# Stick-breaking attention with both heads in one step, half blocks of projections between the steps, and gate projections between the banded units

## The chip, the cores and the metric

The kernel runs on one core of one Trainium2 chip. The metric is the device time of one execution in microseconds (us), taken as the median over runs. A core has five engines that run their own instruction queues in order and wait for one another through semaphores: TensorE (PE, matmuls; its weight loads are shown as PEld), VectorE (DVE), ScalarE (ACT), GpSimd (POOL) and SyncE (SP, which here issues the DMAs). PE writes to PSUM, eight banks of 128 x 512 float32 values.

## The reference

Two transformer blocks follow each other on 1024 positions of width 1024. The first has two layers (banded attention, a gated linear recurrence, memory attention, an MLP each). The change touches only the second block, whose one layer mixes two kinds of attention:

```python
proj = h @ w_in[l]
sb_q, sb_k, sb_v, sb_g, sw_q, sw_k, sw_v, sw_g = jnp.split(proj, offsets, axis=-1)
y_sb = stick_breaking_attention(sb_q, sb_k, sb_v) * jax.nn.silu(sb_g)      # 8 heads of 64
y_sw = sliding_window_sink_attention(sw_q, sw_k, sw_v, sinks) * jax.nn.silu(sw_g)
y = jnp.concatenate([y_sb, y_sw], axis=-1) @ w_out[l]
...
# stick-breaking, s < t only
log_beta = jax.nn.log_sigmoid(z)
log_1mb = jnp.where(causal, jax.nn.log_sigmoid(-z), 0.0)
later = lax.cumsum(log_1mb, axis=3, reverse=True) - log_1mb
w = jnp.where(causal, jnp.exp(log_beta + later), 0.0)
```

## The kernel before

Every tensor that feeds a projection is kept in two float32r parts (high and low), so a projection block (128 output features, all of K = 1024) is 8 x 3 matmuls for each 512 positions: 48 for both halves, 24 for a half block. Weights come in blocks of 512 KB: a DMA into `raw` (`NR` slots), then `split` makes the two parts with an ACT copy and a DVE subtraction into `wsp` (`NS` = 3 slots), two blocks ahead of use (`LA` = 2, called from `piece`). The list `order` gives the order of all blocks.

Nothing reorders the work: `Queues.add` appends each operation to its engine's queue in the order in which the program is written, and each engine executes its queue strictly in that order. An operation's `*after` arguments are the operations that it waits for. So a wait holds whatever is written behind it on the same engine.

Around the change the program of before runs, one stage after the other: projections of the stick-breaking queries (`SQ`), keys (`SK`, 4 blocks), values (`SV`) and gates (`SG`, 4 blocks; the gate is silu through Tanh, line 138 is the ACT helper `A`); a barrier; the stick-breaking steps; a barrier; the projections of the banded queries (`WQ`, 4 blocks), keys (`WK`), values (`WV`) and gates (`WG`, 4 blocks); a barrier; 16 banded units (`attention_units` on `window_units`); and the output projection.

A stick-breaking step of before is one head, one block of 128 keys and up to 512 queries (128, 256 or 384 on the diagonal). There are 96. Its stages, each several steps behind the one before, are: scores z on PE (float32, 64 rows of the array); `min` on DVE; Exp and Ln on ACT; a maximum on DVE, which gives softplus(z); its high part on POOL and low part on DVE; two triangular matmuls that add the sum within the block onto z; two matmuls with a constant matrix (`onesN`) into a carry bank of the head; a copy and an addition, Exp on ACT, and the values matmul (64 columns of the array).

`attention_units` issues for unit u: the scores of u, their maximum on DVE, the Exps; then the normalisation of u-1 (DVE reciprocal, two multiplications on DVE and two on POOL); the values of u-2; the transposes of u-1 and their copies; and last, where `fills[u]` is above 0, a half block from `fill`.

`ln_exp()` loads the ACT table set that holds both Exp and Ln; where a function that the current set lacks comes up, the compiler puts an `ACT_TABLE_LOAD` in front of it.

Of the kernel before, what the change touches and what calls it, by code (L numbers as in the profile page):

```python
# [13 lines left out]
KB = 1024  # L14
# [99 lines left out]
def program(nc, D, out, stop=None, dbg=None):  # L114
    ctx = ExitStack()
    with ctx:
# [34 lines left out]
        NR, NS, LA = 4, 3, 2  # L151
# [58 lines left out]
        blocks("in2", range(26))  # L210
# [135 lines left out]

        def half_chunks(name, bank, rhs, evac):

            def chunk(n, hf):
                b = at[0]  # L350
                assert at[1] == 0
                piece(name)
                cs = slice(512 * hf, 512 * hf + 512)
                ps = PS[:, bank, :]
                for k in range(8):
                    w = wsp[:, b % NS, :, k * 128:k * 128 + 128]
                    rh, rl, ops = rhs(k)
                    for i, (wi, r) in enumerate(((0, rh), (0, rl), (1, rh))):
                        op = mm(ps, w[:, wi, :], r[:, cs], k == 0 and i == 0, k == 7 and i == 2, splits[b], ops,
                                free[bank] if k == 0 and i == 0 else None)  # L360
                if hf == 1:
                    uses[b] = [op]
                    at[0] = b + 1
                free[bank] = [evac(n, cs, ps, op)]

            return [lambda n=n, hf=hf: chunk(n, hf) for n in range(8) for hf in range(2)]
# [348 lines left out]
        def window_units(Qt, Kt, Vt, pairs, tiles, nbs, outf, bias, sinkv):  # L715
            units = []
            for n in range(8):
                for kp in range(pairs):
                    kbs = [n + d for d in nbs if 0 <= n + d < 8]
                    for half in range(2):  # L720

                        def s(j, ps, fr, n=n, kp=kp, kbs=kbs, half=half):
                            m = ps.shape[1] // 2
                            heads = [(par, m * j + t, par * m + t) for t in range(m) for par in range(2)]
                            for par, t, i in heads:
                                rows = slice(64 * par, 64 * par + 64)
                                mm(ps[:, i, :], Qt[rows, kp * tiles + 2 * half + t, n * 128:(n + 1) * 128],
                                   Kt[rows, kp, kbs[0] * 128:(kbs[-1] + 1) * 128], t == m * j, False, fr,
                                   skip_group_check=True)
# [4 lines left out]
                        def pv(pts, ob, fr, n=n, kp=kp, kbs=kbs, half=half):  # L734
                            for j, (pt, c) in enumerate(pts):
                                for par in range(2):
                                    st = Vt[:, kbs[j], kp, 64 * par:64 * par + 64]
                                    o = mm(ob[64 * par:64 * par + 64, 256 * half:256 * half + 256], st,
                                           pt[:, 256 * par:256 * par + 256], j == 0, j == len(pts) - 1, c,
# [499 lines left out]
        SK = place(48 * KB, [128, 4, 1024])  # L1239
        SV = place(64 * KB, [128, 8, 4, 128])  # L1240
        SG = place(0, [128, 4, 1024])
        gt = place(88 * KB, [128, 2, 1024])
        sv_free = [o, *r12[0], *r12[1], *tused]

        project("in2", 4, 8, Hk, copy_to(SK, up1))
        Q.add("act", None, *sv_free)
        project_rows("in2", 4, 8, Hk, rows_to(SV, False, *sv_free))
        for e_ in ("act", "dve"):
            Q.add(e_, None, *sp2)
        gfree = [None, None]  # L1250

        def gate_to(T):
            def ev(n, p, ps, op):
                t = gt[:, n % 2, :]
                a = A(t, ps, ACT.Tanh, op, gfree[n % 2], scale=0.5)
                o = STT(T[:, n, :], t, 1.0, ps, ALU.add, ALU.mult, a)
                gfree[n % 2] = o
                return [o], None
            return ev

        project("in2", 4, 8, Hk, gate_to(SG))
# [3 lines left out]
        me = [place(o_ * KB, [128, 512]) for o_ in (28, 30, 94)]  # L1265
        sps = place(16 * KB, [128, 3, 2, 512], F32R)
        tw = place(88 * KB, [128, 3, 512])
        triI, onesN = triR[:, 0, :], triR[:, 1, :]
        ZB, AB, OBK = (0, 1, 2, 3), (4, 5), (6, 7)
        steps = []  # L1270
        grp = 0
        for pr in range(4):
            for hf in range(2):
                top = 4 * hf + 3
                for kb in range(top, -1, -1):
                    for par in range(2):
                        steps.append((pr, hf, kb, par, top, grp))
                grp += 1
        n_s = len(steps)
        F = [dict() for _ in range(n_s)]  # L1280
        got = lambda s, key: F[s].get(key) if s >= 0 else None

# [288 lines left out]
```

How the kernel before makes its waits and increments, by code:

```python
            def run(eng):  # L93
                seen = {}
                for o in self.q[name]:
                    for d in o.deps:
                        if seen.get(d.sem.name, 0) < d.val:
                            eng.wait_ge(d.sem, d.val)
                            seen[d.sem.name] = d.val
                    if o.fn is None:
                        continue
                    ins = o.fn(eng)
                    if o.sem is not None:
                        ins.then_inc(o.sem, 1 if o.sem is self.sems.get(name) else 16)
```

## Time and profile before

| | us |
|---|---|
| median of 3 runs | 3436.37 (3432.55 to 3443.11) |
| profiled execution, own time | 3448.24 |
| its span, first to last instruction | 3446.5 |
| mean granted TensorE clock over the span | 0.969 |
| steps of stick-breaking, 2830.45 to 3094.24 | 263.8 |
| banded units, 3216.78 to 3341.14 | 124.4 |

In a timeline a row gives the start, the length, the engine, the line, the operation with its output and inputs, and a count; in brackets stands how long the engine had been idle and what released it. Rows of the same kind that follow each other are merged. A float32 matmul appears as two records, a float32r or bfloat16 matmul as one. The granted clock is 1.0 at 2.4 GHz and 0.5 at 1.2 GHz. Line 279 is the matmul helper, 138 the ACT helper, 141, 144, 148 and 149 are DVE helpers; buffers placed by `place` are all called p in the trace.

### The profile page before, as it was taken

The numbers are of one execution on the slowest core, as the hardware profiler recorded it, in microseconds if no ns is written. First come the engines' busy times: TensorE is split into PE (matmuls) and PEld (weight loads), VectorE is DVE, ScalarE is ACT, GpSimd is POOL, SyncE is SP. The second block draws the span as 40 slices with busy tenths as digits, with TensorE's granted clock in tenths as the row PEclk, the third lists the DMA queues.
The fourth block names the chain that finished last, engine by engine and source line by source line (L and its number), as shares of the span: only waits on it lengthen the run. The fifth ranks groups of instructions, "written<-read, shape, count | busy, mean of one in ns | idle before, by whom it ended". The sixth has DMA issues, their size and how long they took to land.

```text
span 3446.5 us, 35176 instructions
## 1 busy us (share of the span) xinstructions
PE 3220.3 (93%) x14288; PEld 2446.3 (71%) x14298; DVE 1706.5 (50%) x2254; ACT 1095.1 (32%) x1853; POOL 261.4 (8%) x258
## 2 busy tenths in 40 slices
PE   4999989999999999999799999999997999999768
PEld 4777557778888888777577788888875874448546
DVE  6544864444444433699644433333345326771355
ACT  4202652311111111488423111111125226761332
POOL 0001431000000000000010000000003002220120
PEclk9999999999999999999899999999998998999799
DMA  4211010122222211211211111111111310001012
GB/s 167 98 37 31 1 56 31 37 74 74 68 73 74 71 46 55 70 46 49 98 37 43 43 49 49 45 48 49 49 50 53 112 37 1 1 19 43 13 68 92
DMA packets 52865, 186.01 MB, mean 54 GB/s; under 512 B 5856, under 2 KB 6240, under 8 KB 52576
## 3 DMA queue, kind: packets, MB, share of 16 engines
q1 hardware_dynamic: 52704, 183.76, 16.2%
q8 instruction: 113, 1.85, 0.2%
q14 instruction: 48, 0.39, 0.0%
HBM read 169.06 MB, written 13.63 MB: 53 GB/s over the span
## 4 chain that ended last, share of the span: by engine, by line
PE 79%; DVE 9%; ACT 7%; issue 2%; POOL 2%; DMA 0%; DVEq 0%; ACTq 0%; POOLq 0%; SPq 0%
PE PS L279 77%; ACT p L138 5%; DVE p L141 3%; PE PS L517 2%; DVE sm L482 1%; DVE p L144 1%; POOL p L508 1%; DVE p L1091 1%; ACT H L138 1%; DVE wsp L141 0%; ACT wsp L138 0%; DVE p L530 0%; ACT L138 0%; DVE p L398 0%; DVE sm L144 0%
## 5 line engine op out<-in xcount | busy, mean ns | idle before, releaser
L279 PE MATMUL PS<-H,wsp 128*128 128x512 f32 x6864 | 1596.5, 393 | 39.7 <-POOL H L1189 21.2
L279 PEld LDWEIGHTS PS<-H,wsp 128*128 128x128 f32 x6864 | 1292.7, 189 | 328.2 <-ACT p L138 25.3
L279 PE MATMUL PS<-p,wsp 128*128 128x512 f32 (+1 forms) x3840 | 896.6, 394 | 42.1 <-DVE p L141 21.6
L279 PEld LDWEIGHTS PS<-p,wsp 128*128 128x128 f32 x3840 | 714.7, 191 | 219.9 <-ACT wsp L138 37.8
L138 ACT ACTIVATE p<-p 128x512 f32<-128x512 f32 (+5 forms) x522 | 355.1, 690 | 860.3 <-DVE p L144 677.3
L138 ACT ACTIVATE wsp<-raw 128x1024 fp32r<-128x1024 f32 (+1 forms) x262 | 271.3, 1039 | 778.0 <-PE PS L279 637.5
L141 DVE TENSOR_TENSOR p<-p,PS 128x1024 f32<-128x1024 f32 (+4 forms) x280 | 251.5, 898 | 505.8 <-PE PS L279 500.0
L141 DVE TENSOR_TENSOR wsp<-raw,wsp 128x1024 fp32r<-128x1024 f32 (+1 forms) x262 | 317.7, 1215 | 200.7 <-ACT wsp L138 200.7
L279 PE MATMUL PS<-p 128*64 128x256 f32 (+9 forms) x1432 | 385.1, 486 | 18.7 <-DVE p L144 5.2
L141 DVE TENSOR_TENSOR p<-PS,p 128x1024 f32<-128x1024 f32 (+1 forms) x124 | 143.0, 1154 | 442.7 <-PE PS L279 417.4
L508 POOL TENSOR_SCALAR p<-p,sm 128x256 f32<-128x256 f32 (+2 forms) x128 | 150.6, 1181 | 1912.1 <-DVE sm L501 1912.1
L141 DVE TENSOR_TENSOR p<-p 128x1024 f32<-128x1024 f32 (+8 forms) x283 | 239.2, 847 | 108.5 <-ACT p L138 106.8
L279 PEld LDWEIGHTS PS<-p 128*64 128x64 f32 (+2 forms) x1432 | 154.5, 177 | 143.4 <-ACT p L138 62.1
L138 ACT ACTIVATE p<-PS 128x512 f32<-128x512 f32 (+4 forms) x245 | 135.6, 573 | 342.1 <-PE PS L279 315.8
L138 ACT ACTIVATE p<-PS,sm 128x256 f32<-128x256 f32 (+2 forms) x256 | 127.9, 508 | 266.9 <-DVE sm L148 137.4
L517 PE MATMUL PS<-cf,p 128*128 128x128 f32 x600 | 97.0, 300 | 77.9 <-POOL p L508 66.0
L144 DVE SCALAR_TENSOR_TENSOR p<-p 128x1024 f32<-128x1024 f32 (+1 forms) x119 | 143.3, 1215 | 20.3 <-ACT p L138 17.8
L517 PEld LDWEIGHTS PS<-cf,p 128*128 128x128 f32 x600 | 72.0, 152 | 114.0 <-issue 63.4
L482 DVE TENSOR_REDUCE sm<-PS 128x2 f32<-128x768 f32 (+3 forms) x96 | 94.9, 989 | 64.8 <-PE PS L279 64.3
L149 DVE TENSOR_SCALAR p<-PS 128x512 f32<-128x512 f32 (+4 forms) x105 | 61.6, 587 | 93.7 <-PE PS L279 93.6
L1341 POOL CAST p<-p 128x512 fp32r<-128x512 f32 (+3 forms) x96 | 69.7, 726 | 344.3 <-ACT p L138 159.6
L279 PE MATMUL PS<-p,triR 128*128 128x512 f32 (+3 forms) x352 | 94.6, 385 | 0.3
(69 smaller groups left out, 1313.7 us busy)
## 6 DMA issues: line engine op xcount, KB each, us to landing
raw<-in_dn_dram SPq DMA_DIRECT2D x68, 512.0 KB, 3.5
raw<-in_in_dram SPq DMA_DIRECT2D x66, 512.0 KB, 3.6
raw<-in_up_dram SPq DMA_DIRECT2D x64, 512.0 KB, 3.6
raw<-in_out_dram SPq DMA_DIRECT2D x40, 512.0 KB, 3.5
p<-in_ada_dram SPq DMA_DIRECT2D x24, 512.0 KB, 4.5
raw<-in_kv_dram SPq DMA_DIRECT2D x16, 512.0 KB, 3.9
p<-in_x_dram SPq DMA_DIRECT2D x16, 512.0 KB, 9.0
spill_dram<-p SPq DMA_DIRECT2D x16, 512.0 KB, 2.9
```

What stands on the lines that cost most here:

```text
L138: return act(lambda e: e.activation(o, i, f, **kw), *a)
L141: return dve(lambda e: e.tensor_tensor(o, x, y, op), *a)
L144: return dve(lambda e: e.scalar_tensor_tensor(out=o, in0=x, scalar=s, in1=y, op0=op0, op1=op1), *a)
L149: return dve(lambda e: e.tensor_scalar(o, x, s1, s2, op0, op1), *a)
L279: return pe(lambda e: e.matmul(o, l, r, start=start, stop=stop, **kw), *a)
L482: o = dve(lambda e: e.tensor_reduce(mx, S, AX.X, ALU.max), op, prev)
L508: last[1] = pool(lambda e, P_=P_, r=r: e.tensor_scalar(P_, P_, r, None, ALU.mult), o)
L517: o = pe(lambda e, t_out=t_out, t_in=t_in: e.transpose(t_out, t_in, ident), probs[J * u + j], free[b])
L1091: L[("h", d)] = dve(lambda e: e.tensor_tensor_scan(out=dst, data0=da, data1=du, initial=0.0, op0=ALU.mult, op1=ALU.add), u, L[("a", d)], y ...
L1341: F[v]["sh"] = pool(lambda e, sh=sh, m=m: e.tensor_copy(sh, m), o, got(v - 3, "carry"), got(v - 3, "cum"))
```

## The change

A step of stick-breaking now is both heads of a pair, so there are 48 of up to 1024 elements in a row. The scores are copied out of PSUM at once (`zc`); the sum within the block and the carry now build up in one pair of banks, `triI` for the block itself and, once the step has been read out, `triS` (its complement) for the rest; the high part is copied by ACT where POOL did it. Of the projections, one block of `SK`, `SV`, `WK` and `WV` stay ahead of the steps (`WK` and `WV` go to HBM and come back); the 4 blocks of `SG`, 3 of `SK` and the 4 of `WQ` become 22 half blocks, one after every second step. Of `WG`, two half blocks run ahead of the banded units and six between them. `NR` goes from 4 to 3.

```diff
-        NR, NS, LA = 4, 3, 2
+        NR, NS, LA = 3, 3, 2
...
+        t_bufs = [place(o_ * KB, [128, 2, 512]) for o_ in (80, 84, 88)]
+        m_bufs = [place(o_ * KB, [128, 2, 512]) for o_ in (24, 28)]
+        ZB, PB, OBK = 0, 2, (4, 5)
+        steps = [(pr, hf, kb) for pr in range(4) for hf in range(2) for kb in range(4 * hf + 3, -1, -1)]
...
+        def fill_gate(T, slot, done, *after):
+            def ev(cs, ps, op):
+                a = A(T[:, slot, cs], ps, ACT.Tanh, op, *after, scale=0.5)
+                o = STT(T[:, slot, cs], T[:, slot, cs], 1.0, ps, ALU.add, ALU.mult, a)
+                done[cs.start // 512] = o
+                return o
+            return ev
+
+        def fill_query(t):
+            return lambda cs, ps, op: dve(lambda e: e.tensor_copy(WQ[:, t, cs], ps), op)
...
+        work = [gate(0), lambda: fill_keys(1), gate(1), lambda: fill_keys(2), gate(2), lambda: fill_query(0),
+                lambda: fill_keys(3), gate(3), *(lambda t=t: fill_query(t) for t in (1, 2, 3))]
+        work = [lambda i=i, f=f, hf=hf: half_chunk("in2", 6 + i % 2, Hk, f(), hf, hf == 1)
+                for i, (f, hf) in enumerate((f, hf) for f in work for hf in range(2))]
...
+        def pe_within(s):
...
+            for part, op in ((sh, F[s]["sh"]), (sl, F[s]["sl"])):
+                for par in range(2):
+                    o = mm(pb[:, par, :], triI, part[:, par, :], False, False, op, skip_group_check=True)
+        def pe_carry(s):
...
+                for part in (sh, sl):
+                    for par in range(2):
+                        o = mm(pb[:, par, :], triS, part[:, par, :], False, False, F[s]["add"], skip_group_check=True)
...
-        for s in range(n_s + 6):
...
+        for s in range(n_s + 3):
+            if 0 <= s - 3:
+                pe_carry(s - 3)
+            if 0 <= s - 2 < n_s:
+                pe_within(s - 2)
+            if s < n_s:
+                pe_scores(s)
+            if 0 <= s - 3:
+                pe_values(s - 3)
+            if s % 2 == 0 and work:
+                work.pop(0)()
+            v, u = s - 1, s - 2
             if 0 <= v < n_s:
+                o = A(m, m, ACT.Exp, F[v]["min"])
+                o = A(m, m, ACT.Ln, o, bias=1.0)
+                F[v]["m"] = STT(m, t, 0.125, m, ALU.mult, ALU.max, o)
+            if s < n_s:
+                F[s]["zc"] = A(t, z, ACT.Copy, F[s]["qk"], got(s - 3, "pv"))
+                free[ZB] = free[ZB + 1] = [F[s]["zc"]]
+            if 0 <= u < n_s:
+                F[u]["add"] = TT(t, t, pb, ALU.add, F[u]["cum"], F[u]["m"])
+            if s < n_s:
+                F[s]["min"] = TS(m, t, 0.125, 40.0, ALU.mult, ALU.min, F[s]["zc"], got(s - 2, "sl"), got(s - 2, "sh"))
             if 0 <= v < n_s:
+                F[v]["sh"] = A(sh, m, ACT.Copy, F[v]["m"], got(v - 2, "carry"))
+                F[v]["sl"] = TT(sl, m, fz(sh), ALU.subtract, F[v]["sh"], got(v - 2, "carry"))
+            if 0 <= u < n_s:
+                F[u]["w"] = A(t, t, ACT.Exp, F[u]["add"], scale=0.125)
...
+        wkl = Q.dma(None, WK[:, 0, :], D["wk"], wk_out, *ends)
+        wbl = Q.dma(None, wb_raw[:, :, :], D["swb"], *ends)
+        wvl = Q.dma(None, WV[:, :, 0, :], D["wv"], wv_out, *ends)
...
+        for _ in range(2):
+            work.pop(0)()
         wbl = A(wb[:, :, :], wb_raw[:, :, :], ACT.Copy, wbl)
...
-        attention_units(units, 256, 80 * KB, 0.125, True)
+        attention_units(units, 256, 80 * KB, 0.125, True, work, [1, 1, 0, 1, 0, 1, 0, 1, 0, 1] + [0] * 8)
```

How the queues come out is shown at three places. First ACT in the steps of full width, before. p72 to p74 hold softplus, p76 takes z and then the weights; each `x2` is Exp and Ln of a step.

```order
L138 ACTIVATE p72<-p72 128x512 x2
L138 ACTIVATE p76<-p76 128x512
L138 ACTIVATE p76<-PS 128x512
L138 ACTIVATE p73<-p73 128x512 x2
L138 ACTIVATE p76<-p76 128x512
L138 ACTIVATE p76<-PS 128x512
L138 ACTIVATE p74<-p74 128x512 x2
```

Then ACT after, at a gate's half block: p77 and p78 are the `m` buffers (Exp, then Ln in place), p79 and p80 the high parts, p74 to p76 the `t` buffers (copy of z, later Exp of the weights), p71 is the gate `SG`.

```order
L138 ACT_TABLE_LOAD
L138 ACTIVATE p75<-p75 128x1024
L138 ACTIVATE p71<-PS 128x512
L138 ACTIVATE p78<-p78 128x1024
L138 ACT_TABLE_LOAD
L138 ACTIVATE p78<-p78 128x1024
L138 ACTIVATE p75<-PS 128x1024
L138 ACTIVATE p80<-p78 128x1024
L138 ACT_TABLE_LOAD
```

Two table loads now stand in every step, one ahead of each Ln and one ahead of the Exp of the weights, and the gate's Tanh (p71) stands ahead of the next step's Exp and Ln. Between row 686 and the end of the steps the queue of after holds 98 rows of ACT_TABLE_LOAD, the same stage before holds 1.

PE before, where a wide step meets a narrow one: p75 is the high and low part, p67 and p68 are `SQ` and `SK`, p76 and p69 the weights and `SV`.

```order
L279 MATMUL PS<-p76,p69 64x512
L279 MATMUL PS<-cb 128x512
L279 MATMUL PS<-p67,p68 128x128
L279 MATMUL PS<-cb 128x128
L279 MATMUL PS<-p75,triR 128x512 x4
L279 MATMUL PS<-p76,p69 64x512
```

PE after, a step of full width with its half block: p79 and p80 high parts, p81 and p82 low parts, p75 the weights, `H,wsp` the half block.

```order
L283 MATMUL PS<-p80,triR 128x512 x2
L283 MATMUL PS<-p82,triR 128x512 x2
L283 MATMUL PS<-p79,triR 128x512 x2
L283 MATMUL PS<-p81,triR 128x512 x2
L283 MATMUL PS<-p67,p68 128x512 x2
L283 MATMUL PS<-p75,p70 64x512 x2
L283 MATMUL PS<-H,wsp 128x512 x24
```

The scores of the two heads now follow each other (`x2`), and so do their values; the same matmuls are issued as in two steps of before, and a half block of 24 stands behind every second step.

DVE after, at the same gate's half block: p71 is the gate, p81 and p82 the low parts.

```order
L141 TENSOR_TENSOR p81<-p77,p79 128x1024
L144 SCALAR_TENSOR_TENSOR p71<-p71,PS 128x512
L144 SCALAR_TENSOR_TENSOR p78<-p74,p78 128x1024
L141 TENSOR_TENSOR p76<-p76,PS 128x1024
L149 TENSOR_SCALAR p77<-p75 128x1024
L141 TENSOR_TENSOR p82<-p78,p80 128x1024
```

The gate's product stands ahead of the maximum of the next step (p78) and of the addition (p76) that PE's carry waits for.

## Rows read from the trace of the kernel before

**Rows 1.** The page, parts 1 and 4: busy share of each engine; chain of waits by engine.
```profile
PE 3220.3 (93%) x14288; PEld 2446.3 (71%) x14298; DVE 1706.5 (50%) x2254; ACT 1095.1 (32%) x1853; POOL 261.4 (8%) x258
...
PE 79%; DVE 9%; ACT 7%; issue 2%; POOL 2%; DMA 0%; DVEq 0%; ACTq 0%; POOLq 0%; SPq 0%
```

**Rows 2.** Windows by stage: start:end, length, busy time and count per engine, granted clock.
```profile
2782.25:2830.45 48.20, 45.43 (x193) 37.19 (x194) 9.52 (x8) 8.88 (x10) 0.00 (x0) 0.96 0.14 44
2830.45:3094.24 263.79, 259.24 (x816) 112.32 (x824) 193.67 (x392) 187.27 (x385) 69.74 (x96) 0.94 0.00 1
...
3170.58:3216.78 46.20, 43.74 (x194) 35.95 (x194) 10.41 (x12) 9.96 (x13) 0.00 (x0) 1.00 0.15 46
3216.78:3341.14 124.36, 74.56 (x433) 45.82 (x433) 65.32 (x146) 49.26 (x172) 30.36 (x32) 0.80 0.00 1
```

**Rows 3.** Timeline of PE, one one-head step of full width: start, length, count.
```profile
2947.01 1.20 PE L279 MATMUL PS<-p,triR 128*128 128x512 f32 x4
2948.14 2.12 PE L279 MATMUL PS<-p 128*64 128x512 f32 x4
```

**Rows 4.** Timeline of PE in the banded units at full clock.
```profile
3283.84 1.14 PE L279 MATMUL PS<-p 64*128 64x256 f32 x8
...
3285.45 1.08 PE L279 MATMUL PS<-p 128*64 128x256 f32 x8
3289.69 1.06 PE L517 MATMUL PS<-cf,p 128*128 128x128 f32 x8 [3.15 <-POOL p L508]
```

**Rows 5.** Lines by form, whole span: count, busy us, mean ns of one.
```profile
L141 DVE TENSOR_TENSOR p<-p,PS 128x1024 f32<-128x1024 f32 x136 | 166.0, 1221 | 407.5 <-PE PS L279 407.5
L144 DVE SCALAR_TENSOR_TENSOR p<-p 128x1024 f32<-128x1024 f32 x118 | 143.1, 1224 | 20.3 <-ACT p L138 17.8
...
L138 ACT ACTIVATE p<-PS 128x512 f32<-128x512 f32 x152 | 87.6, 598 | 87.1 <-PE PS L279 60.9 <-PE PS L517 26.0
L138 ACT ACTIVATE p<-p 128x1024 f32<-128x1024 f32 x82 | 85.8, 1057 | 83.1 <-DVE p L141 76.0 <-DVE p L149 6.5
...
L530 DVE COPY p<-PS 128x512 f32<-128x512 f32 x62 | 42.5, 686 | 23.3 <-PE PS L517 23.3
...
L138 ACT ACTIVATE p<-p 128x256 f32<-128x256 f32 x58 | 23.8, 413 | 5.1 <-DVE p L149 3.6 <-DVE p L398 0.5
L138 ACT ACT_TABLE_LOAD x17 | 21.8, 1283 | 1.0 <-PEq L1557 0.7
...
L148 DVE TENSOR_SCALAR p<-p 128x1024 f32<-128x1024 f32 x7 | 4.9, 693 | 0.2
```

**Rows 6.** Timeline of ACT around two table loads.
```profile
1465.33 0.62 ACT L138 ACTIVATE wsp<-raw 128x512 fp32r<-128x512 f32 x1
1465.96 1.28 ACT L138 ACT_TABLE_LOAD   x1
1467.25 2.01 ACT L138 ACTIVATE p<-p 128x1024 f32<-128x1024 f32 x2
...
2782.54 1.28 ACT L138 ACT_TABLE_LOAD   x1
2795.08 1.03 ACT L138 ACTIVATE p<-PS 128x1024 f32<-128x1024 f32 x1 [11.26 <-PE PS L279]
```

**Rows 7.** Timeline of all engines, one banded unit from its scores to its transposes.
```profile
3285.56 1.23 DVE L482 TENSOR_REDUCE sm<-PS 128x4 f32<-128x1024 f32 x1 [0.92 <-PE PS L279]
...
3287.56 1.98 POOL L508 TENSOR_SCALAR p<-p,sm 128x256 f32<-128x256 f32 x2 [4.86 <-DVE sm L501]
```

**Rows 8.** Windows: the start of the one-head steps, and after it.
```profile
2830.00:2864.00 34.00, 32.72 (x77) 15.80 (x79) 15.35 (x38) 16.26 (x39) 4.89 (x10) 0.51 0.00 1
2865.00:2900.00 35.00, 34.96 (x108) 14.34 (x107) 28.08 (x52) 26.22 (x50) 10.70 (x13) 1.00 0.00 1
```

**Rows 9.** Timeline of PE, first matmul of the one-head steps.
```profile
2830.45 0.65 PE L279 MATMUL PS<-p 64*128 64x128 f32 x2 [2.77 <-DVE p L144]
```

**Rows 10.** DMA issues between 3080 and 3346: KB each, us to landing.
```profile
p<-in_swb_dram SPq DMA_DIRECT2D x1, 1024.0 KB, 5.6
```

More of the change, by code:

```diff
@@ L209, in program @@
         blocks("in2", range(4))
-        blocks("in2", range(26))
+        blocks("in2", range(4))
+        blocks("in2", (20, 21, 4, 8, 9, 10, 11))
+        blocks("in2", (12, 5, 13, 6, 14, 16, 7, 15, 17, 18, 19))
+        blocks("in2", (22, 23, 24, 25))
+        blocks("in2", (22, 23, 24, 25))
         blocks("out2", range(8))
@@ new lines, in pe_carry, with pe_values @@
+        def pe_carry(s):
+            c0, z, t, m, sh, sl, pb = view(s)
+            if steps[s][2] > 0:
+                for part in (sh, sl):
+                    for par in range(2):
+                        o = mm(pb[:, par, :], triS, part[:, par, :], False, False, F[s]["add"], skip_group_check=True)
+                F[s]["carry"] = o
+            else:
+                p_open[:] = [F[s]["add"], F[s]["add"]]
+                F[s]["carry"] = F[s]["cum"]
+        def pe_values(s):
+            pr, hf, kb = steps[s]
+            c0, z, t, m, sh, sl, pb = view(s)
+            ob = OBK[hf]
+            if kb == 4 * hf + 3:
+                mm(PS[:, ob, :], zerob, cb[:, 0:512], True, False, c_cb, free[ob], skip_group_check=True)
+            for par in range(2):
+                o = mm(PS[64 * par:64 * par + 64, ob, c0:512], SV[:, kb, pr, 64 * par:64 * par + 64], t[:, par, :],
+                       False, False, F[s]["w"], skip_group_check=True)
@@ new lines, in program @@
+            if 0 <= u < n_s:
+                c0, z, t, m, sh, sl, pb = view(u)
+                F[u]["w"] = A(t, t, ACT.Exp, F[u]["add"], scale=0.125)
+        assert not work
+        for par in range(2):
+            free[PB + par] = [p_open[par]]
+        ends = Q.barrier()
+        WK = place(56 * KB, [128, 1, 1024])
+        WV = place(60 * KB, [128, 8, 1, 128])
+        wkl = Q.dma(None, WK[:, 0, :], D["wk"], wk_out, *ends)
+        WG = place(64 * KB, [128, 4, 1024])
+        wb = place(92 * KB, [128, 8, 256], BF16)
@@ L1385, in program @@
-        project_rows("in2", 1, 8, Hk, rows_to(WV, False))
-        project("in2", 4, 8, Hk, gate_to(WG))
-        Q.barrier()
+        xl3 = {k: Q.dma(None, X[:, k, :], D["spill"][:, k, :], sp2[k], wbl, *ends) for k in (0, 1, 6, 7)}
         def bias2(n, kbs, t, par, ps):
@@ L1400, in out2 @@
             return [o]
-        units = window_units(WQ, WK, WV, 1, 4, (-1, 0), out2, bias2, lambda name, kp, half: V(name + "2", 4 * half, 4))
+        units = window_units(WQ, WK, WV, 1, 4, (-1, 0), out2, bias2, lambda name, kp, half: V(name + "2", 4 * half, 4),
+                             wkl, wvl)
         for k in range(4):
-            units[3 + 3 * k]["side"] = lambda k=k: to_parts(lambda _: SQ[:, k, :], lambda _: Hk(k), 1)
-        attention_units(units, 256, 80 * KB, 0.125, True)
-        Q.barrier()
+            units[10 + k]["side"] = lambda k=k: to_parts(lambda _: SQ[:, k, :], lambda _: Hk(k), 1, chunk[7])
+        attention_units(units, 256, 80 * KB, 0.125, True, work, [1, 1, 0, 1, 0, 1, 0, 1, 0, 1] + [0] * 8)
+        assert not work
         ends = Q.barrier()
         ln_exp()
-        xl3 = [Q.dma(None, X[:, k, :], D["spill"][:, k, :], sp2[k], *ends) for k in range(8)]
+        for k in range(2, 6):
+            xl3[k] = Q.dma(None, X[:, k, :], D["spill"][:, k, :], sp2[k], *ends)
         Hops[:] = [None] * 8
```

219 lines of the change are left out of this document (86 added, 133 removed).

## The prediction

> **What bounds the kernel now.** I read the page first. PE is busy 93% of the span and holds 79% of the chain of waits [rows 1], so what counts is how much PE works and how long it stands. Then the windows by stage [rows 2]: the one-head steps take 263.8 us with PE busy 259.2, while DVE is busy 194 and ACT 187. PE bounds the steps, and the other engines have room of about a quarter. A gate projection of 4 blocks is 43.74 us of solid PE, so a block costs 10.94 us and a half block 5.47. The banded units are the other kind of stage: 124.4 us with PE busy 74.6. The timeline gives the price of a one-head step of full width [rows 3]: 4 float32r matmuls in 1.20 us, then values and scores in 2.12 us, a period of 3.2 us. Last come the costs per operation on ACT and DVE [rows 5] and the table loads [rows 6].
>
> **What the change does to PE.** No matmul goes away. Moved into the steps are 4 gate blocks, 3 key blocks and 4 query blocks, 11 blocks or 22 half blocks. Before, these and the steps took 263.8 + 11 x 10.94 = 384.1 us, and with one stage fewer a wait between two stages goes (2.8 us behind the gates: 48.20 less 45.43 [rows 2]; I take 2.4), together 386.5 us. That is the number to beat.
> PE gets cheaper work. Where two half-array matmuls stand back to back, the banded units show them side by side: four float32 scores of 256 columns take 1.14 us and four values matmuls 1.08 us [rows 4], 1024 columns each. Two of 512 columns are the same 1024 columns, so I take 1.1 us for the two heads' scores and 1.1 for their values; before, the same work was two steps of 2.12 us [rows 3]. The bound from above is that 2 x 2.12 = 4.2, from below 2.2. The 8 float32r matmuls take 2.0 to 2.4 us (2 x 1.20). A full two-head step then is 4.3 us of PE against 6.4. With widths of 128, 256, 384 and six times 512 for two heads (4608 columns a pair of heads, 36 full steps in all) PE's work falls by some 75 us. If PE still set the pace, this would be a large gain.
>
> **What it does to ACT and DVE.** The instruction order of after shows two things that decide against that. First, Tanh now lies among the steps, and the table set that holds both Exp and Ln is left for good: every step has one ACT_TABLE_LOAD ahead of Ln and one ahead of the Exp of the weights, 96 in all where the stage had one. A load is 1.28 us [rows 5], and the operation behind it starts 0.01 us after its end [rows 6], so I take 1.30 each. The load itself does not wait for the input of the operation behind it: one ran at 2782.54, its Tanh at 2795.08 [rows 6]. So it is hidden where ACT idles, but not where ACT is the chain.
> The Trainium skill, page "ScalarE: Activation LUTs", section "What ACT_TABLE_LOAD costs", gives a switch as the load plus a drain of about 1380 ns, 2.66 us in all; the trace has the next ACTIVATE 0.01 us behind the load, so the sum stays with the row. By the page the 96 loads would cost up to 132 us more, and a rival below has a chance for something of that kind.
> Second, the half block's evacuation is put into the queues of ACT and DVE ahead of the softplus of the next step. ACT cannot begin Exp and Ln of step s-1 until Tanh has its half block, and DVE cannot do the maximum and then the addition until the copy of a key or query half block is done. PE's next carry waits for that addition. The work that should hide behind the half block stands behind it.
>
> **One filled pair of steps, full width, at full clock.** Prices [rows 5]: ACT on 1024 elements 1.06, DVE 1.22 (two inputs) and 0.69 (the min), Tanh on 512 elements 0.60, copy of a half block on DVE 0.69, a load 1.30, a handover about 0.1. I count from the end of the maximum of one step to that of the step after the next.
> Odd step (no half block), along ACT: 0.1 + high part 1.06 + load 1.30 + weights 1.06 + Exp 1.06 + load 1.30 + Ln 1.06 + 0.1 + maximum 1.22 = 8.2 us. PE's 4.3 us is hidden in it.
> Even step: the low part is ready at 0.1 + 1.22 (addition) + 0.69 + 1.22 = 3.3, its two matmuls 0.5, scores 1.1, values 1.1, which makes 6.0; then the half block 5.47, 11.5 in all. Behind a key or query half block come 0.1 + 0.69 + 1.22 = 2.0; behind a gate's 0.1 + 0.60 + 1.06 + 1.30 + 1.06 + 0.1 + 1.22 = 5.4.
> So a pair takes 21.7 us with keys or queries, 25.1 with gates, 16.4 without. Narrow operations shrink (0.41 us at 256 elements [rows 5]), loads and the half block do not: with about 0.52 and 0.95 us for a mean operation on ACT, and DVE alike, the odd step is 5.3 and 7.6 us, the even one 3.1 and 5.5 before its half block and 1.4 and 1.9 behind it, so the pair of widths 128 and 256 takes 15.3 us and that of 384 and 512 takes 20.5. A pair of heads has two of each: 2 x (15.3 + 20.5 + 21.7) = 115. Four of them 460; 8 gates add 3.4 each, 27; the last two pairs have no half block, 11 less; filling and draining the pipeline 12. That is 488 us. Where a narrow step meets a wide one the operations of a chain belong to different steps and some of both chains overlap, which I put at 20 us: 468.
>
> **The clock.** At the start of the one-head steps PE had idled 2.77 us [rows 9] and the granted clock then was 0.51 for 34 us, 1.00 after [rows 8]; the banded units, with PE busy 60%, ran at 0.80 [rows 2]. The new stage is of the banded kind: PE works some 280 us of 470, with idle stretches of 3 to 5 us around each half block. A half block at 1.2 GHz takes 5.47 us more. If about a quarter of its work and of the odd steps' falls into such stretches, it costs 27 us; the bounds are 0 and 22 x 5.47 = 120. Steps and half blocks then take 495 us: 108 us more than the 386.5.
>
> **The banded units.** A unit's cycle runs from its scores over the maximum (1.23 us), the reciprocal and the multiplications on POOL (1.98) [rows 7] to the transposes, for which PE idles 3.15 us [rows 4]. A half block is queued behind the transposes and ahead of the next scores, so that chain starts only when it is done. It covers nothing, and the six cost 6 x 5.47 as before, like the two ahead of the units. DMA: the bias comes as 1024 KB, which took 5.6 us [rows 10], behind 512 KB of keys, and is hidden by the two half blocks; its conversion on ACT stands behind their Tanhs, about 2 us of PE idle. Against it go one barrier's wait (46.20 less 43.74 [rows 2]) and part of the clock lost in the units. I take -5 us, between -15 and +10.
> `NR` = 3 costs nothing: three blocks of `raw` last at least 3 x 5.47 = 16 us of matmuls, while a transfer of twice a block's size took 5.6 us [rows 10]. The trip of `WK` and `WV` through HBM ends long before its use. POOL loses its casts, which nothing waited for in length. The earlier `spill` loads change nothing on the path.
>
> **Sum.** The profiled execution was 3448.2 us; + 108 - 5 = 3551. It was 12 us above the median of the runs shown, so I predict 3540.
>
> **The rivals.**
> *ACT's work alone sets the pace (faster).* If Tanh and the copies find their half blocks finished and PE's work hides, the stage is ACT's busy time: per full step 5 x 1.06 + 2 x 1.28 = 7.9 us, 4.6 at 128, 5.7 at 256, 6.8 at 384; per pair of heads 2 x (4.6 + 5.7 + 6.8) + 6 x 7.9 = 81.6, times 4, and 16 for splits and Tanhs: 343 us, 43 less than 386.5. The time would be 3390. It decides as soon as a filled pair of full width takes under 17 us. For it: ACT before ran with only short waits. Against: the order of the queues, which is strict. Chance 0.05.
> *The paired matmuls do not run side by side.* Each full step has 2 us more PE; in the odd steps ACT covers it, in the 22 even ones some 1.6 us show: 35 us more, 3575. Against it [rows 4]. Chance 0.12.
> *A table load holds ACT for longer than its record.* Twice as long (1.3 us more), of which some 80% on the chain, is 96 x 1.3 x 0.8 = 100 us: 3640. The row speaks against it. Chance 0.06.
> *The clock stays at 2.4 GHz* because every half block is solid work: 27 us less, 3513. Chance 0.15.
> *The loads hide and only the queue order is left.* Without 4 x 1.30 us a pair takes some 5 us less than with them on the chain, half of it then refilled by PE: 24 x 2.5 = 60 us less, 3480. Chance 0.05.
> The forecast itself has 0.57, with a range of its own of 3505 to 3580.
>
> **How the numbers follow.** What a measurement can tell from no change is 0.3%, 10 us around 3436. Faster: the first rival, 0.05. Same: 0.02, a tail of the last rival. Slower: all else, 0.93. The range goes from 3480 (last rival) to 3600 (paired matmuls and a poorer clock together); outside lie the first rival, the long loads and a few per cent of tails.
>
> **What would show it.** In the profile after: 95 more ACT_TABLE_LOAD of 1.28 us; the stage from the first score to the last value near 495 us, with PE busy under 65% of it and ACT near 340 us; PE waiting for DVE at the carry, longest after the gates' half blocks, 5 to 7 us; two scores of 512 columns in about 1.1 us; a filled pair of 20 to 25 us; a granted clock of 0.8 to 0.95; banded units with the same 3 us gap behind each POOL multiplication. I am wrong if Exp and Ln of the next step run beside the half block, if PE is busy over 80% of the stage, or if the banded units get shorter by more than 15 us than 124.4 + 43.7.

## The result and the profile after

| us | before | after |
|---|---|---|
| median (lowest to highest of 4 runs each) | 3438.07 (3432.55 to 3443.11) | 3563.09 (3556.26 to 3569.69) |
| profiled execution, own time | 3448.24 | 3564.15 |
| its span | 3446.5 | 3562.3 |
| mean granted clock over the span | 0.969 | 0.950 |

The changed kernel is slower: ratio 1.0364, 95% interval 1.0338 to 1.0390. The prediction was 3540 (3480 to 3600).

The page, parts 1 and 4, of the kernel after (before: [rows 1]): busy share of each engine, and the chain of waits by engine.

```profile
PE 3207.7 (90%) x14280; PEld 2452.8 (69%) x14298; DVE 1687.0 (47%) x2088; ACT 1220.2 (34%) x1809; POOL 191.7 (5%) x162
...
PE 73%; ACT 11%; DVE 10%; issue 3%; POOL 2%; DMA 0%; DVEq 0%; ACTq 0%; POOLq 0%; SPq 0%
```

PE works 13 us less, the span is 116 us longer, and ACT has gone from 7% to 11% of the chain. The loss lies in two stretches. Windows of the kernel after: from the first score of the steps to their last value, and from the first of the gates' half blocks ahead of the banded units to the units' end (start:end, length, busy time and count of PE, PEld, DVE, ACT and POOL, granted clock).

```profile
2782.00:3276.50 494.50, 359.51 (x1336) 213.35 (x1352) 186.49 (x234) 331.95 (x357) 0.00 (x0) 0.83 0.04 12
3276.74:3455.54 178.80, 125.50 (x624) 86.54 (x625) 80.58 (x162) 63.63 (x189) 30.36 (x32) 0.84 0.14 48
```

The first stretch runs from 2782.24 to 3275.86: 493.6 us for what took 386.5, 107 more. The second is 178.8 us against 46.2 + 124.4 = 170.6 of before [rows 2], the gates' block with the wait behind it and the units: 8.2 more. Together 115 us; the spans differ by 116.

Lines by form in the steps of the kernel after, 2782 to 3276 (count | busy us, mean ns | idle before, and what ended it; a lower clock makes PE's means longer):

```profile
L283 PE MATMUL PS<-H,wsp 128*128 128x512 f32 x528 | 135.6, 415 | 0.0
L138 ACT ACT_TABLE_LOAD x97 | 124.5, 1283 | 1.7
...
L283 PE MATMUL PS<-p,triR 128*128 128x512 f32 x160 | 63.3, 544 | 48.1 <-DVE p L141 47.9
...
L283 PE MATMUL PS<-p,triR 128*128 128x384 f32 x64 | 22.1, 465 | 34.1 <-DVE p L141 34.0
...
L283 PE MATMUL PS<-p,triR 128*128 128x256 f32 x64 | 15.9, 369 | 14.3 <-DVE p L141 13.7
L283 PE MATMUL PS<-p,triR 128*128 128x128 f32 x64 | 13.6, 326 | 24.3 <-DVE p L141 21.2 <-ACT p L138 2.9
```

PE idles ahead of the triangular matmuls for 121 us, and DVE's line 141 ends 117 of them. That helper makes two things, the addition that the carry waits for and the low part; by what ran last on DVE before each wait ended, some 113 us belong to the addition and 4 to the low part. The half blocks (528 matmuls, 22 x 24) themselves never wait. The next two extracts show such a wait, first on PE and then on the engines that it waits for. PE's timeline around two gates' half blocks of the kernel after:

```profile
2858.68 6.92 PE L283 MATMUL PS<-H,wsp 128*128 128x512 f32 x24
2871.72 3.34 PE L283 MATMUL PS<-p,triR 128*128 128x384 f32 x8 [6.12 <-DVE p L141]
...
2882.22 2.14 PE L283 MATMUL PS<-p 64*128 64x512 f32 x8
2884.29 5.75 PE L283 MATMUL PS<-H,wsp 128*128 128x512 f32 x24
2896.43 3.78 PE L283 MATMUL PS<-p,triR 128*128 128x512 f32 x8 [6.39 <-DVE p L141]
```

And the first of them on ACT and DVE (timeline of all engines, the same kernel):

```profile
2865.63 0.60 ACT L138 ACTIVATE p<-PS 128x512 f32<-128x512 f32 x1 [9.29 <-PE PS L283]
2866.13 1.05 ACT L138 ACTIVATE p<-p 128x1024 f32<-128x1024 f32 x1
2866.26 0.69 DVE L144 SCALAR_TENSOR_TENSOR p<-p,PS 128x512 f32<-128x512 f32 x1 [8.66 <-ACT p L138]
2867.19 1.28 ACT L138 ACT_TABLE_LOAD   x1
2868.49 1.06 ACT L138 ACTIVATE p<-p 128x1024 f32<-128x1024 f32 x1
...
2869.58 1.23 DVE L144 SCALAR_TENSOR_TENSOR p<-p 128x1024 f32<-128x1024 f32 x1 [2.63 <-ACT p L138]
2870.72 0.95 DVE L141 TENSOR_TENSOR p<-p,PS 128x768 f32<-128x768 f32 x1
```

Read it downwards: Tanh can start only when the half block is done (2865.63); ACT had been idle for 9.29 us. Behind it follow Exp, the load, Ln, on DVE the maximum and the addition, and then PE's carry at 2871.72. The input of that Exp comes from DVE, which had been idle for 8.66 us, so it had been ready for at least that long; Exp stood behind Tanh in the queue. The row at 2882.22 shows the other side: scores and values of two heads, 512 wide, in 2.14 us together, where before each head took 2.12 [rows 3].

### The profile page after: what moved, and what is told of

It reads as the page before. It is cut to its first block, busy times and chain, and to the rows that moved or that the text cites. A ratio compares the mean times of both kernels' runs of the same rounds, so it can differ in the third digit from the quotient of the medians.

```text
span 3562.3 us, 34777 instructions
## 1 busy us (share of the span) xinstructions
PE 3207.7 (90%) x14280; PEld 2452.8 (69%) x14298; DVE 1687.0 (47%) x2088; ACT 1220.2 (34%) x1809; POOL 191.7 (5%) x162
## 4 chain that ended last, share of the span: by engine, by line
PE 73%; ACT 11%; DVE 10%; issue 3%; POOL 2%; DMA 0%; DVEq 0%; ACTq 0%; POOLq 0%; SPq 0%
PE PS L283 71%; ACT p L138 8%; DVE p L141 4%; PE PS L523 2%; DVE p L144 2%; ACT L138 2%; DVE sm L488 1%; POOL p L514 1%; DVE p L1097 1%; ACT H L138 1%; ACT wsp L138 0%; DVE wsp L141 0%; DVE p L536 0%; DVE sm L144 0%; DVE p L149 0%
## 5 line engine op out<-in xcount | busy, mean ns | idle before, releaser
L283 PE MATMUL PS<-H,wsp 128*128 128x512 f32 x6864 | 1619.4, 396 | 38.3 <-POOL H L1195 21.2
L283 PE MATMUL PS<-p,wsp 128*128 128x512 f32 (+1 forms) x3840 | 896.7, 394 | 42.1 <-DVE p L141 21.7
L138 ACT ACTIVATE p<-p 128x1024 f32<-128x1024 f32 (+7 forms) x426 | 364.8, 872 | 920.7 <-DVE p L144 758.7
L141 DVE TENSOR_TENSOR p<-p,PS 128x1024 f32<-128x1024 f32 (+2 forms) x232 | 244.3, 1053 | 502.6 <-PE PS L283 502.6
L283 PE MATMUL PS<-p 128*64 128x256 f32 (+9 forms) x1432 | 319.5, 513 | 19.0 <-ACT p L138 5.9
L141 DVE TENSOR_TENSOR p<-p 128x1024 fp32r<-128x1024 f32 (+5 forms) x235 | 232.3, 991 | 109.4 <-ACT p L138 107.3
L144 DVE SCALAR_TENSOR_TENSOR p<-p 128x1024 f32<-128x1024 f32 (+3 forms) x167 | 189.2, 1140 | 134.8 <-ACT p L138 132.2
L283 PE MATMUL PS<-p,triR 128*128 128x512 f32 (+3 forms) x352 | 111.0, 458 | 120.8 <-DVE p L141 116.7
L138 ACT ACTIVATE p<-PS 128x512 f32<-128x512 f32 (+4 forms) x198 | 121.2, 637 | 273.8 <-PE PS L283 247.1
L283 PEld LDWEIGHTS PS<-p 128*64 128x64 f32 (+2 forms) x1432 | 135.2, 186 | 115.0 <-issue 73.6
L283 PEld LDWEIGHTS PS<-p,triR 128*128 128x128 f32 x352 | 72.9, 246 | 160.0 <-DVE p L141 146.6
```

The costliest lines, as they stand in the source:

```text
L138: return act(lambda e: e.activation(o, i, f, **kw), *a)
L141: return dve(lambda e: e.tensor_tensor(o, x, y, op), *a)
L144: return dve(lambda e: e.scalar_tensor_tensor(out=o, in0=x, scalar=s, in1=y, op0=op0, op1=op1), *a)
L283: return pe(lambda e: e.matmul(o, l, r, start=start, stop=stop, **kw), *a)
```

## The experiments

A difference in us to another run ("less than after") compares the medians; every ratio is to the kernel before on the same chip, whose median was 3434 to 3440 us from chip to chip.

### 1 and 2. The table loads

Experiment 1 loads the set with Exp and Ln again behind each Tanh; 96 loads become 16.

```diff
             a = A(T[:, slot, cs], ps, ACT.Tanh, op, *after, scale=0.5)
+            if T is SG:
+                ln_exp()
```

> The changed kernel with one addition: behind every Tanh of a gate half block in the steps the set with Exp and Ln is loaded again, so the 96 loads of the steps become 16 (two around each of 8 Tanhs). Theory (the order of the queues costs most, the loads about a third of the loss): the chain of a step gets 2.6 us shorter, but PE's work, the half block and its evacuation still stand in a row; the stage of steps goes from 493.6 us to 460 (435 to 475), the time from 3563 to 3530 (3505 to 3545). Rival (the loads are nearly the whole loss): the stage falls to about 386, the time to 3455. Rival (a load is hidden where ACT idles anyway): no change, 3560.

Measured: 3548.82 us (3539.77 to 3555.99), ratio 1.0319 (1.0295 to 1.0343): 14 us less than after, where 33 were expected; it lies outside the range that was given.

Experiment 2 has no function outside the set, and so no load. Its gate is another function; only its time is of use.

```diff
-            a = A(T[:, slot, cs], ps, ACT.Tanh, op, *after, scale=0.5)
+            a = A(T[:, slot, cs], ps, ACT.Tanh if T is not SG else ACT.Exp, op, *after, scale=0.5)
```

> The changed kernel with Exp in place of Tanh in the stick-breaking gates' half blocks, so that this part of the computation is another function, and no table load is left among the steps. It costs the same 0.6 us on ACT. Theory: like the reload, with 16 loads less on the way behind gate half blocks: 3520 (3500 to 3540); the difference to the reload is at most 16 x 1.3 = 21 us. If the reload and this one differ by more, a load costs more than its 1.28 us.

Measured: 3527.46 us (3522.67 to 3534.33), ratio 1.0251 (1.0228 to 1.0275): 36 us less than after. In its steps PE still idles for over 100 us (window, columns as above):

```profile
2782.00:3240.00 458.00, 354.44 (x1357) 208.95 (x1358) 190.68 (x235) 205.55 (x264) 0.00 (x0) 0.87 0.04 13
```

ACT is busy for only 205 us of 458, and still PE waits. So the loads are a smaller cause, 36 of the 107 us. Removing 80 of them saves 14 us, and removing the 16 around the Tanhs saves 21 more. These 21 are as much as 16 loads of 1.28 us last, but they are not all load time. In experiment 1 a load ahead of Tanh runs while ACT waits for the half block anyway, and only the 8 behind a Tanh stand in the way, 10 us. Between the two traces PE's idle time in the steps falls by 8 us (from 109 to 101) and its busy time, for the same 1352 records, by 15 (from 368.4 to 353.3), at a granted clock of 0.82 in experiment 1 and 0.87 here. So most of the 21 is clock. Where the other 80 loads hide was not followed.

At 0.37 us saved per load, the rival in which a load holds ACT for twice its record falls. So does the estimate of up to 132 us more, which the prediction had from the Trainium skill's figure for the drain (page "ScalarE: Activation LUTs", section "What ACT_TABLE_LOAD costs"); in the timeline above Ln starts 0.02 us behind its load. The rule of the same page's section "Table sets: the hidden batching unit", that one set has both Exp and Ln and that calls are to be batched by set, agrees: without Tanh no load is left among the steps.

### 3 and 4. The place of the half block's evacuation in the queues

Experiment 3 changes nothing on PE. The Tanh, product or copy that empties a half block's bank is queued behind the step's own operations on ACT and DVE.

```diff
+            if later is not None:
+                later.append(lambda: free.__setitem__(bank, [evac(cs, ps, op)]))
+                return op
...
                 F[u]["w"] = A(t, t, ACT.Exp, F[u]["add"], scale=0.125)
+            while later:
+                later.pop(0)()
```

> The changed kernel with the evacuation of a half block (Tanh and product, or copy) queued behind all operations of its step on ACT and DVE, not ahead of them; all table loads stay. Theory: Exp, Ln and the maximum of the next step now run beside the half block's 5.5 us of matmuls, the stage falls from 493.6 to about 390 us, where ACT's chain of 8.2 us a step sets the pace; the time is 3460 (3440 to 3490). Rival (loads are the main cause): the order matters little, 3540 or more.

Experiment 4 is this and the reload of experiment 1.

> Both edits: evacuation queued behind the step, and the Exp and Ln set loaded again behind each Tanh. Theory: the stage is 335 to 365 us, between PE's work of about 285 at full clock and what the chain of a step needs; the time is 3425 (3405 to 3450), under the kernel before if the granted clock stays above 0.95. If PE's cheaper paired matmuls were not real the stage would be 380 or more.

Measured: experiment 3 3448.04 us (10 runs, 3442.56 to 3453.33), ratio 1.0024 (1.0012 to 1.0036), 115 us less than after; experiment 4 3438.00 us (10 runs, 3428.41 to 3445.01), ratio 0.9990 (0.9975 to 1.0005). Both lie in their ranges. The steps of experiment 3, and then of experiment 4 (windows):

```profile
2782.00:3165.00 383.00, 326.73 (x1348) 200.36 (x1348) 186.73 (x232) 331.49 (x357) 0.00 (x0) 0.89 0.05 16
```

```profile
2782.00:3137.00 355.00, 309.09 (x1323) 185.63 (x1322) 187.62 (x231) 221.22 (x272) 0.00 (x0) 0.93 0.05 15
```

With the loads and all other work unchanged, the steps of experiment 3 take 383 us instead of 494. PE idles for 56 us instead of 135, and the same matmuls are busy for 33 us less at a clock of 0.89 instead of 0.83. How a half block now hides the chain (timeline of all engines, experiment 3):

```profile
2876.36 5.74 PE L283 MATMUL PS<-H,wsp 128*128 128x512 f32 x24
2876.50 1.28 ACT L138 ACT_TABLE_LOAD   x1
...
2877.79 1.06 ACT L138 ACTIVATE p<-p 128x1024 f32<-128x1024 f32 x1
...
2878.89 1.23 DVE L144 SCALAR_TENSOR_TENSOR p<-p 128x1024 f32<-128x1024 f32 x1 [2.09 <-ACT p L138]
2880.03 1.21 DVE L141 TENSOR_TENSOR p<-p,PS 128x1024 f32<-128x1024 f32 x1
...
2881.93 2.02 PE L283 MATMUL PS<-p,triR 128*128 128x512 f32 x8
2882.50 0.69 DVE L1285 COPY p<-PS 128x512 f32<-128x512 f32 x1
```

Load, Ln, maximum and addition run beside the half block, the carry follows it without a gap, and the copy comes last, when nothing waits for it. The main cause is shown by this: the order of the queues. The 80 loads that the reload saves are then worth 10 us more (experiment 4 against 3).

### 5 and 6. The gates' half blocks and the banded units

Experiment 5 runs all eight ahead of the units and none between.

```diff
-        for _ in range(2):
+        for _ in range(8):
...
-        attention_units(units, 256, 80 * KB, 0.125, True, work, [1, 1, 0, 1, 0, 1, 0, 1, 0, 1] + [0] * 8)
+        attention_units(units, 256, 80 * KB, 0.125, True)
```

> The changed kernel with all eight half blocks of the banded gates ahead of the units, none between them. Theory (between the units a half block covers nothing, since it stands ahead of the next unit's scores, and it keeps the units from the steady pace that before reached at full clock): the units and the eight half blocks, 178.8 us in the changed kernel, take 169 (165 to 176), the time 3553 (3545 to 3562). Rival (they hide some of PE's waits there): 10 to 20 us longer, 3575 or more.

Experiment 6 puts six of them behind a unit's scores and normalisation and ahead of its values and transposes: a negative entry takes the place that a value above 1 has in the code.

```diff
-                    if fill and fills[u] > 1:
+                    if fill and (fills[u] > 1 or fills[u] < 0):
...
-        attention_units(units, 256, 80 * KB, 0.125, True, work, [1, 1, 0, 1, 0, 1, 0, 1, 0, 1] + [0] * 8)
+        attention_units(units, 256, 80 * KB, 0.125, True, work, [0, -1, 0, -1, -1, -1, -1, -1] + [0] * 10)
```

> The changed kernel with the six half blocks put behind the next unit's scores and ahead of the values and transposes, where PE waits 3.15 us for POOL. Theory: each covers up to that wait, 6 x 3 = 18 us less, and PE idles less: 3540 (3530 to 3552). Rival (the wait only moves to another place, because DVE and ACT have the evacuation queued ahead of the normalisation): no change, 3560.

Measured: experiment 5 3550.99 us (3548.89 to 3558.93), ratio 1.0333 (1.0318 to 1.0348), 12 less than after, as expected; experiment 6 3523.19 us (3511.76 to 3527.5), ratio 1.0249 (1.0232 to 1.0266), 40 less, where 23 were expected, 18 of them as covered waits. PE's timeline in the kernel after, a half block and the transposes and scores behind the next wait, at half clock:

```profile
3324.10 6.36 PE L283 MATMUL PS<-H,wsp 128*128 128x512 f32 x24
...
3336.24 1.94 PE L523 MATMUL PS<-cf,p 128*128 128x128 f32 x8 [3.15 <-POOL p L514]
3338.11 2.08 PE L283 MATMUL PS<-p 64*128 64x256 f32 x8
```

The same in experiment 6, then its lines from 3277 to 3416, and its window:

```profile
3317.02 5.70 PE L283 MATMUL PS<-H,wsp 128*128 128x512 f32 x24
3322.65 1.08 PE L283 MATMUL PS<-p 128*64 128x256 f32 x8
3323.66 1.09 PE L523 MATMUL PS<-cf,p 128*128 128x128 f32 x8
3324.69 1.13 PE L283 MATMUL PS<-p 64*128 64x256 f32 x8
```

```profile
L283 PE MATMUL PS<-H,wsp 128*128 128x512 f32 x192 | 46.1, 396 | 2.3 <-DVE p L144 2.3
...
L523 PE MATMUL PS<-cf,p 128*128 128x128 f32 x120 | 17.1, 287 | 29.6 <-POOL p L514 29.6
```

```profile
3276.70:3416.30 139.60, 104.00 (x624) 72.61 (x625) 80.19 (x163) 63.18 (x189) 30.21 (x32) 0.96 0.17 61
```

Lines of the kernel after from 3277 to 3455:

```profile
L283 PE MATMUL PS<-H,wsp 128*128 128x512 f32 x192 | 51.3, 427 | 2.3 <-DVE p L144 2.3
L523 PE MATMUL PS<-cf,p 128*128 128x128 f32 x120 | 23.9, 363 | 47.3 <-POOL p L514 47.3
```

In experiment 6 this stretch takes 139.3 us instead of 178.8. Waits for POOL before the transposes fall from 47.3 to 29.6 us, which is 18 of the 40: the half block now covers the wait. The rest, 21.5 us, goes with the clock, 0.96 instead of 0.84: the same 624 matmuls are busy for 104.0 us instead of 125.5, the transposes among them 17.1 instead of 23.9, the half blocks 46.1 instead of 51.3. The expectation counted the covers and took the clock for small. In experiment 5 the units start on 45 us of half blocks at a clock of 1.00:

```profile
3276.00:3321.00 45.00, 35.64 (x150) 26.76 (x148) 11.48 (x12) 10.04 (x13) 0.00 (x0) 1.00 0.33 117
3321.00:3448.00 127.00, 74.69 (x474) 48.15 (x476) 68.03 (x149) 53.74 (x177) 30.19 (x32) 0.91 0.07 25
```

Half blocks at full clock, but from the second on each waits 1.4 to 1.5 us for the product that empties the one bank they share (bank 7).

### 7. NR = 3 alone, in the kernel before

```diff
-        NR, NS, LA = 4, 3, 2
+        NR, NS, LA = 3, 3, 2
```

> The kernel before with NR = 3 alone. Theory: no load comes later than it is used, no change, 3438 (3430 to 3446), ratio 1.000 within 0.002. Rival (the shorter ring costs at the start, where eight loads of x stand ahead of the fourth block): 3 us or more.

Measured: 3434.00 us (12 runs), ratio 0.9997 (0.9985 to 1.0008). It costs nothing, as predicted.

### 8. All three remedies

The kernel after with the late evacuation, the reload and the place of experiment 6.

> Late evacuation, reload of the Exp and Ln set, and the six banded half blocks ahead of the transposes. Theory: the gain of the late evacuation with reload (to 3438) and that of the banded half blocks (18 us) add, 3420 (3408 to 3432), faster than the kernel before. Rival (the gains overlap through the clock): 3435.

Measured: 3397.61 us (3394.34 to 3400.43), ratio 0.9888 (0.9876 to 0.9901), 22 better than expected, 1.1% faster than before and faster than the kernel after. The expectation took 18 us for the place of the half blocks, and experiment 6 had given 40; that difference is the 22. Its steps, and its half blocks and banded units (windows):

```profile
2782.00:3147.90 365.90, 316.81 (x1335) 193.15 (x1348) 188.49 (x232) 224.83 (x276) 0.00 (x0) 0.92 0.05 16
3148.78:3291.16 142.38, 106.79 (x624) 74.53 (x625) 80.04 (x162) 64.56 (x190) 30.21 (x32) 0.95 0.18 60
```

Against before that is 386.5 - 365.9 = 21 us in the steps and 170.6 - 142.4 = 28 us in the second stretch; the spans (3446.5 and 3398.0) differ by 48.5. The profiled execution of before was a long one, 14 us above the median of before's runs on this chip (3434.38), so by the medians the gain is 37 us. Profiles of the same stage differ too: the steps of experiment 4 are the same program and took 355 us in its profile, 10 us below its median.

### 9. The gate without Tanh

Experiment 8 without its 16 loads: silu through Exp, a reciprocal on DVE and a product.

```diff
+                    a = A(x, ps, ACT.Exp, op, *after, scale=-1.0)
+                    o = TS(x, x, 0.5, 0.5, ALU.mult, ALU.add, a)
+                    o = dve(lambda e: e.reciprocal(x, x), o)
+                    o = TT(x, x, ps, ALU.mult, o)
```

> The kernel with all three edits, and the stick-breaking gate by Exp, an addition, a reciprocal and a product, the same function without Tanh, so no table load is left in the steps: 16 loads less on ACT, two VectorE operations of 512 more behind each gate half block. With late evacuation the 80 loads less of the reload had been worth 10 us, so 16 are worth 2: 3396 (3388 to 3402). If the loads around a Tanh are worth more than others, as the 21 us between the reload and the Exp gate say, it is 3380 to 3388.

Measured: 3416.69 us (3406.28 to 3420.26), ratio 0.9933 (0.9909 to 0.9956): 19 us slower than experiment 8 (15 by the ratios), not equal or faster. The line that the expectation left out (lines by form, DVE):

```profile
L1296 DVE RECIPROCAL p<-p 128x512 f32<-128x512 f32 x8 | 26.8, 3353 | 0.3
```

A reciprocal of 512 elements in a row takes 3.35 us, five times a copy of the same size (0.69 [rows 5]), and it stands in the queue that the carry waits for. In DVE's timeline one reciprocal runs from 2868.60 to 2871.95, the next step's maximum and addition start only behind it, at 2872.60 and 2873.73, and PE's carry starts at 2875.00 after a wait of 3.60 us. The steps take 387 us in this profile, 366 in that of experiment 8. Sixteen loads of 1.28 us on ACT are cheaper than eight of these.

### 10. The pairing of the heads' matmuls

Experiment 8 with a head's values issued between the two heads' scores, so that no two half-array matmuls of a kind follow each other.

```diff
+                if par:
+                    half_values(s - 3, 0)
```

> The kernel with all three edits, and in each step the scores and values of the two heads issued in turn (scores, values, scores, values), so that no two half-array matmuls of one kind stand side by side. Theory (the two heads' matmuls run side by side, which takes 2.1 us from a full step): the 22 filled steps get 2.1 us longer at full width, the others partly: 50 us more, 3448 (3430 to 3475). Rival (pairing is worth nothing, the gain is elsewhere): 3398.

Measured: 3483.43 us (3480.5 to 3500.68), ratio 1.0142 (1.0115 to 1.0169), 86 us more than experiment 8, where some 50 were expected. PE's timeline (scores and values merged in one row), and the window of the steps without their last 16 us:

```profile
2869.11 4.18 PE L283 MATMUL PS<-p 64*128 64x512 f32 x8
```

```profile
2782.00:3229.00 447.00, 416.92 (x1322) 223.46 (x1322) 184.31 (x229) 216.94 (x271) 0.00 (x0) 0.86 0.04 13
```

4.18 us instead of 2.14: 2.04 us a step, and with the width of 36 full steps 73 us of PE work, about the 75 that the prediction had for the pairing. PE fills 93% of this window, so PE sets the pace here. The other 13 us are not traced further; the clock was 0.86 here and 0.92 in experiment 8.

### 11. The gates' part alone, in the kernel before

Before with its one-head steps, two half blocks of `WG` ahead of the units and six between, placed as in experiment 6.

```diff
-        project("in2", 4, 8, Hk, gate_to(WG))
-        Q.barrier()
+        work = [lambda t=t, hf=hf: chunk.append(half_chunk("in2", 7, Hk, fill_gate(t), hf, True))
+                for hf in range(2) for t in range(4)]
+        for _ in range(2):
+            work.pop(0)()
...
+        attention_units(units, 256, 80 * KB, 0.125, True, work, [0, -1, 0, -1, -1, -1, -1, -1] + [0] * 10)
```

> The kernel before with the second part of the change alone, in its better place: two of the banded gates' half blocks ahead of the units, six between the scores and the transposes. Theory: the gate projection and the units, 170.6 us, become about 140 as in the run with the half blocks in that place: 3404 (3396 to 3412), so of what the kernel with all three edits gains over before (37 us) this part is 30 and the steps 7. Rival (the gain was only what the changed kernel had lost there): 3425 or more.

Measured: 3412.75 us (3409.25 to 3418.04), ratio 0.9930 (0.9910 to 0.9950). That is 24 us less than before by the ratio (27 by the medians), where 30 were expected; the median lies just above the range that was given (3396 to 3412). So this part gives about 0.7% of the 1.1% of experiment 8. If the parts add, the two-head steps with their 22 half blocks, most of the change, give the other 0.4% or so, and only with the evacuation queued late: without it no run with two-head steps was faster than before.

## Why the prediction was right, and where it was not

**The step that decides was right: the work that should hide behind the half block stands behind it.** 495 us were predicted for the steps, 493.6 came. The pairs by which it was summed are in PE's timeline of the kernel after, as starts of half blocks: two pairs of full width with queries, then two narrow ones with keys.

```profile
2991.31 5.75 PE L283 MATMUL PS<-H,wsp 128*128 128x512 f32 x24
...
3013.66 5.78 PE L283 MATMUL PS<-H,wsp 128*128 128x512 f32 x24
...
3035.13 5.74 PE L283 MATMUL PS<-H,wsp 128*128 128x512 f32 x24
...
3052.98 5.73 PE L283 MATMUL PS<-H,wsp 128*128 128x512 f32 x24
...
3071.51 6.39 PE L283 MATMUL PS<-H,wsp 128*128 128x512 f32 x24
```

22.4 and 21.5 us (predicted 21.7), then 17.9 and 18.5 (predicted 15.3 and 20.5, so the first was too low and the second too high by 2 or more, and the sum was right). After the gates' half blocks at 2858.68 and 2884.29 it was 25.6 and 24.7 (predicted 25.1), with waits at the carry of 6.12 and 6.39 us (predicted 5 to 7). Experiment 3 shows the cause by removing it: -115 us.

**The loads** were right in number (97 in the stage) and length (1.28 us), but the sum charged too much for them. It put all of them on the chain, which by the prediction's own rival was worth 60 us; removing all 96 saved 36 us (experiment 2), and 80 of them 14 (experiment 1). The sum came out right all the same, so other terms made up for it, and that part is luck.

**The paired matmuls** ran side by side as predicted: 2.14 us for what was put at 2 x 1.1, and experiment 10 gives the value in the whole kernel, 86 us. So the change's gain is real. It was given back as waits.

**ACT's busy time** was 332 us in the steps (near 340 predicted). The rival in which ACT's work alone sets the pace (343 us) came nearest in experiment 3, where ACT is busy for 331 of 383 us. That is still 40 us above 343, but 111 below the kernel after: the order of the queues was what ruled that rival out.

**PE's share was wrong.** Under 65% was predicted, 73% came (359.5 of 494.5). The work was judged about right, some 280 us at full clock: the same matmuls are busy for 309 us at a clock of 0.93 in experiment 4. The clock was not: at 0.83 they are busy for 50 us more than there (a few us of that difference are uncertain, since the traces hold 1336 and 1323 of the 1348 records). The 22 half blocks account for some 9 us of it, taking each at the 5.74 us that 15 of them show.

**The terms "-20 us of overlap, +27 of clock"** came right as a sum: 488 us stood there without the two, 495 with them, 493.6 were measured. Their sizes are not borne out. The four pairs of full width with queries took 22.4, 21.5, 22.8 and 20.9 us at granted clocks of 0.77, 0.84, 0.90 and 0.92, on average 21.9, where the prediction had 21.7 at full clock; a clock term of 27 us would have made each some 1.1 longer. So in these pairs the clock cost less on the path than was put down. How much the overlap gave back no run separates.

**The banded units were mis-sized**: -5 us was predicted (between -15 and +10), +8.2 came, 13 more. The waits for POOL stayed at 47.3 us, as said. What the step left out is that in before the 43.7 us of gates were steady work at full clock [rows 2]. Cut into eight and put between the units they took 51.3 us, 7.6 more. About 2 of these are the cut itself, since a single half block takes 5.7 us at a clock of 1.00 too (experiment 5; 8 x 5.7 = 45.7); the other 5.6 come with the units' lower clock. The conversion of the bias costs PE 1.84 us (2 predicted), and the one bank shared by the half blocks 1.41 us at the second of them, not foreseen; the barrier gives 2.5 back. That sums to 8.4 for the 8.2.

**The total** is 23 us low. For the profiled execution 3551 was predicted, and it took 3564.15, 13 more: the units cost 13 more than predicted and the steps 1 less. The other 10 us come from the step to the median: before's profiled execution was above its median and I took 12 us off, but after's was 1 us above its own.

## What to carry to other kernels

Filler work between the steps of a pipeline goes into every engine's queue, not only into PE's: queue its evacuation behind the step's own operations on ACT and DVE, or the operations that it should cover wait for it (115 us here). Put filler on PE between the start of a chain and the wait that ends it, not behind that wait (40 us here, 18 of them waits and the rest a higher clock). When a new function joins a loop, count the table loads in the instruction order of the whole loop: eight half blocks' Tanhs among 48 steps brought 96 loads.

## What the runs showed of the hardware

- Half-array float32 matmuls of 512 columns, two of a kind issued one behind the other: scores and values of two heads in 2.14 us. The same four alternated: 4.18 us (experiment 10), both at full clock.
- With the alternated ones PE was busy for 93% of the steps and yet the granted clock was 0.86, lower than the 0.92 of experiment 8 with PE busy 87%. From 3190 to 3226 PE was busy for 34.35 of 36 us, at a clock of 0.53. A high busy share on the page did not go with a high clock.
- The 16 banded units had a clock of 0.79 in before and 0.90 in experiment 5, with the same work and projections at 1.00 ahead of them both times. From their first scores to their last matmul they took 122.1 us in before and 114.6 in experiment 5. What decides it was not found.
- A DVE reciprocal of 128 x 512 float32 takes 3.35 us, a copy of that size 0.69.
- A table load runs ahead of the wait of the operation behind it: in experiment 1 one ran at 2854.41, and the Tanh behind it started at 2863.47, when its half block was done.
